# Products of ones in TensorE's first waits, bias and sink products later, and one rounding moved on ScalarE, in an encoder block

## The reference

```
h = modulate(rmsnorm(x, g0), sh1, sc1);  x = x + 0.5 * g1 * swiglu(h, w_ffn1_in, w_ffn1_out)
h = modulate(rmsnorm(x, g1), sh2, sc2);  x = x + g2 * (concat(hgrn2(h), attention(h)) @ w_mix_out)
h = modulate(rmsnorm(x, g2), sh3, sc3);  x = x + 0.5 * g3 * swiglu(h, w_ffn2_in, w_ffn2_out)
```

## Time and profile before

| | |
|---|---|
| median of 3 runs | 1033.9 us |
| lowest and highest | 1032.92 and 1034.93 us |
| the profiled execution | 1033.38 us |
| its span, first to last instruction | 1031.6 us |
| TensorE matmul busy | 1012.9 us, 98% |
| TensorE weight loads busy | 897.5 us, 87% |
| VectorE busy | 802.1 us, 78% |
| ScalarE busy | 507.8 us, 49% |
| GpSimd busy | 44.2 us, 4% |

### The profile page before, as it was taken

How to read it: one execution, slowest core, us unless ns; L and a number is a source line. 1 busy time by engine, 2 the same in 40 slices (tenths; PEclk the granted TensorE clock), 3 DMA queues, 4 the chain that set the end, 5 groups by cost and what they waited for, 6 DMA issues and landing times.

```text
span 1031.6 us, 16712 instructions
## 1 busy us (share of the span) xinstructions
PE 1012.9 (98%) x6238; PEld 897.5 (87%) x6238; DVE 802.1 (78%) x1189; ACT 507.8 (49%) x782; POOL 44.2 (4%) x32
## 2 busy tenths in 40 slices
PE   5999999999999999999999999999999999999998
PEld 3788999999888888888888888887999999988887
DVE  6889989988988789878788649578988888746533
ACT  4646555555222354683526773454655555532231
POOL 0000000000000050000200000420000000000000
PEclk9999999999999999999999999999999999999999
DMA  9643434343777442832120031222233332363312
GB/s 344 235 163 123 136 110 141 106 159 126 289 279 246 165 163 82 268 100 83 41 72 31 2 83 41 82 82 82 87 117 101 102 121 82 124 245 128 116 41 82
DMA packets 93811, 133.59 MB, mean 130 GB/s; under 512 B 10786, under 2 KB 77214, under 8 KB 93639
## 3 DMA queue, kind: packets, MB, share of 16 engines
q1 hardware_dynamic: 93438, 130.83, 37.9%
q10 hardware_dynamic: 328, 2.17, 0.6%
HBM read 130.88 MB, written 4.21 MB: 131 GB/s over the span
## 4 chain that ended last, share of the span: by engine, by line
PE 87%; DVE 7%; POOL 2%; DMA 2%; ACT 1%; issue 1%; SPq 0%; POOLq 0%; DVEq 0%; ACTq 0%
PE bank L2038 13%; PE bank L2039 13%; PE bank L2040 13%; PE bank L2286 11%; PE bank L2285 11%; PE bank L2284 11%; PE bank L2388 2%; DVE w_lo L1252 2%; PE bank L2489 2%; PE bank L2582 1%; PE bank L2475 1%; PE bank L2175 1%; DVE tmod L1336 1%; PE bank L2161 1%; PE bank L2167 1%; PE bank L2464 1%
## 5 line engine op out<-in xcount | busy, mean ns | idle before, releaser
L755 ACT ACTIVATE w_hi<-w_raw 128x2048 fp32r<-128x2048 f32 x47 | 89.9, 1913 | 202.1 <-PE bank L2040 191.2
L1252 DVE TENSOR_TENSOR w_lo<-w_raw,w_hi 128x2048 fp32r<-128x2048 f32 x47 | 109.5, 2330 | 94.7 <-ACT w_hi L755 94.7
L2284 PE MATMUL bank<-t_hi,left_hi 128*128 128x256 f32 x544 | 154.0, 283 | 0.0
L2285 PE MATMUL bank<-t_lo,left_hi 128*128 128x256 f32 x544 | 154.0, 283 | 0.0
L2286 PE MATMUL bank<-t_hi,left_lo 128*128 128x256 f32 x544 | 153.9, 283 | 0.0
L2038 PE MATMUL bank<-a_hi,w_hi 128*128 128x512 f32 x352 | 137.7, 391 | 0.3 <-DVE w_lo L1252 0.3
L2040 PE MATMUL bank<-a_hi,w_lo 128*128 128x512 f32 x352 | 137.0, 389 | 0.0
L2039 PE MATMUL bank<-a_lo,w_hi 128*128 128x512 f32 x352 | 137.0, 389 | 0.0
L2038 PE MATMUL bank<-h_hi,w_hi 128*128 128x512 f32 x336 | 133.3, 397 | 0.8 <-DVE w_lo L1252 0.8
L2040 PE MATMUL bank<-h_hi,w_lo 128*128 128x512 f32 x336 | 130.9, 390 | 0.0
L2039 PE MATMUL bank<-h_lo,w_hi 128*128 128x512 f32 x336 | 130.8, 389 | 0.0
(11 more groups left out here) (313 smaller groups left out, 1898.2 us busy)
## 6 DMA issues: line engine op xcount, KB each, us to landing
w_raw<-in_w_ffn_in SPq DMA_DIRECT2D x42, 1024.0 KB, 4.9
ada<-in_w_ada SPq DMA_DIRECT2D x24, 1024.0 KB, 5.0
w_raw<-in_w_ffn_out SPq DMA_DIRECT2D x22, 1024.0 KB, 4.9
w_raw<-in_w_mix_in SPq DMA_DIRECT2D x11, 1024.0 KB, 5.1
shift_in<-in_w_ada SPq DMA_DIRECT2D x4, 1024.0 KB, 8.3
ada_row<-in_w_ada SPq DMA_DIRECT2D x8, 512.0 KB, 4.1
scale_in<-in_w_ada SPq DMA_DIRECT2D x4, 512.0 KB, 6.8
x_nat<-in_x SPq DMA_DIRECT2D x2, 1024.0 KB, 8.6
```

The source lines that it names most:

```text
L755: sc.activation(w_hi[n % 2][:], src[:], ACT.Copy).then_inc(whi_done, 1)
L1252: ve.tensor_tensor(w_lo[n % 2][:], src[:], as_f32(w_hi[n % 2][:]), ALU.subtract).then_inc(wlo_done, 1)
L2284: te.matmul(into, wh, xh[:, k, :], start=(opens and k == 0), stop=False, skip_group_check=True)
L2285: te.matmul(into, wh, xl[:, k, :], start=False, stop=False, skip_group_check=True)
```

## The change

It has three parts.

1. A function `spin(n)` on TensorE multiplies the tile of ones by itself, the moving side repeated to 512 columns, n times into bank 6, whose content nobody reads. It is called with 2 at the start (after `ones` is filled), with 7 after the transpose of c, with 3 between the first and second token halves of x's transposes, and with 4 ahead of xn's transposes: 16 float32 products in all.
2. The bias and sink products move from ahead of xn's transposes to behind the products of the first two tiles of h. The wait for the copy of bank 0 (`vec_step`) goes, since the sink product now writes to columns 480 to 487 of bank 7. The transposes of xn 3 and x 2 now stand ahead of the second column sums, and these wait for the copied sink.
3. On ScalarE the rounding of the first half of weight tile 0 stands ahead of `evac_x(0)`, and the copy to `sink_b` moves behind `first_t(1)`.

```diff
--- before.py
+++ after.py
@@ -409,6 +409,7 @@
         def sum_bank(u):
             return bank[u]
 
+        SINK_SUM = bank[7][:, 480:480 + QH]
         LOW_D = 6
         LOW_BANK, CROSS_BANK = bank[LOW_D], bank[7]
 
@@ -802,15 +803,15 @@
             sc.activation(rms0[:, 1, :], rms0[:, 0, :], ACT.Sqrt, bias=eps_t[:], scale=1.0 / D).then_inc(norms[0].rt, 1)
             a.wait_ge(norms[0].rinv, 1)
             sc.activation(xn[:, 0, :], x_nat[:, 0, :], ACT.Copy, scale=rms0[:, 2, 0:1]).then_inc(norms[0].rt, 1)
-            a.wait_ge(sink_step, 1)
-            sc.activation(sink_b[:], bank[0][:, 0:QH], ACT.Copy).then_inc(sink_step, 1)
-            evac_x(0)
             a.wait_ge(first_ready[6], 16)
             sc.activation(w_hi[0][:, 0:4 * 2 * P], w_first[0][:, 0:4 * 2 * P], ACT.Copy).then_inc(first_split, 1)
+            evac_x(0)
             first_hi(0)
             first_hi(1)
             first_t(0)
             first_t(1)
+            a.wait_ge(sink_step, 1)
+            sc.activation(sink_b[:], SINK_SUM, ACT.Copy).then_inc(sink_step, 1)
             a.wait_ge(bias_mm, 1)
             sc.activation(row8[:], bank[3][0:QH, :], ACT.Copy).then_inc(rowpad_done, 1)
             evac_x(1)
@@ -2104,8 +2105,16 @@
                                     start=True, stop=True)
                 ins.then_inc(nm.wsum, 1)
 
+            def spin(n):
+
+                for _ in range(n):
+                    te.matmul(bank[6][:], ones[:], ones[:].unsqueeze(1).to_broadcast([P, 4, P]), start=True, stop=True)
+
+            pe.wait_ge(pool_set, 2)
+            spin(2)
             pe.wait_ge(consts_loaded, 32)
             te.transpose(bank[2][:, 0:DT], c_row[:], ident[0:DT, 0:DT]).then_inc(c_step, 1)
+            spin(7)
 
             def turn(dst, src, d, rows=range(TT)):
                 for t in rows:
@@ -2134,14 +2143,11 @@
             turn(bank[1], x_nat, 0, (0, 1))
             pe.wait_ge(c_step, 2)
             turn(bank[2], x_nat, 1, (0, 1))
+            spin(3)
             pe.wait_ge(x_loaded[1], 16)
             turn(bank[1], x_nat, 0, (2, 3)).then_inc(x_tr, 1)
             turn(bank[2], x_nat, 1, (2, 3)).then_inc(x_tr, 1)
-
-            pe.wait_ge(bias_consts, 48)
-            pe.wait_ge(vec_step, 2)
-            te.matmul(bank[3][0:QH, :], relb[:], table[:], start=True, stop=True).then_inc(bias_mm, 1)
-            te.matmul(bank[0][:, 0:QH], ones[0:1, :], sink_r[:], start=True, stop=True).then_inc(sink_step, 1)
+            spin(4)
             pe.wait_ge(norms[0].rt, 2)
             for rows_done, part in ((1, (0, 1)), (2, (2,)), (3, (3,))):
                 pe.wait_ge(xn_done, rows_done)
@@ -2176,18 +2182,21 @@
                                         start=False, stop=(k == DT - 1))
                 return ins
 
-            pe.wait_ge(sink_step, 2)
             pe.wait_ge(xT_act, 1)
             pe.wait_ge(first_split, 1)
             hi_hi(0, (0, 1))
             pe.wait_ge(first_split, 2)
             lo_hi(0, (0, 1))
             hi_lo(0, (0, 1))
-            column_sums(16, quarter_acc[1], 2, 2)
+            pe.wait_ge(bias_consts, 48)
+            te.matmul(bank[3][0:QH, :], relb[:], table[:], start=True, stop=True).then_inc(bias_mm, 1)
+            te.matmul(SINK_SUM, ones[0:1, :], sink_r[:], start=True, stop=True).then_inc(sink_step, 1)
             pe.wait_ge(norms[0].t, 1)
             turn_xn(3)
             pe.wait_ge(norms[0].t, 2)
             turn_x(2)
+            pe.wait_ge(sink_step, 2)
+            column_sums(16, quarter_acc[1], 2, 2)
             hi_hi(0, (2, 3))
             lo_hi(0, (2, 3))
             hi_lo(0, (2, 3))
```

## The result

| | before | changed |
|---|---|---|
| median | 1033.99 us (20 runs) | 1035.32 us (20 runs) |
| ratio | | 1.0013, 95% interval 1.0007 to 1.0019 |
| profiled execution | 1033.38 us, span 1031.6 | 1035.02 us, span 1033.2 |

The changed kernel is 1.3 us slower: less than the 0.2% that the forecast called the bound, but clear of the interval. The forecast was 1035.0. As the experiments show, part of that agreement is luck: one term was too small, and something that I had not seen gave 0.6 us back. One further execution of the kernel before, beside e1 to e4, took 1249.7 us at a mean granted clock of 0.76 and is left out of all figures.

What follows compares the result with a forecast made beforehand. TensorE, busy for 98% of the span, was taken to bound the kernel. At ScalarE's first tile of h, 16.7 + r/2 + 1.4 - 18.65 with r = 3.3 gave +1.1 us: 1035.0 us, range 1032.4 to 1037.4.

Steps and rivals of the forecast that it cites:

- The price of a product: One product of ones on TensorE takes 0.86 us at the high clock level, 1.72 at the low.
- the queue: TensorE works in order; 16 products (13.76 us) and 1.8 to 1.9 of transposes and sums precede xn's transposes.
- the sum: Delay of ScalarE's first tile of h: 16.7 + r/2 + 1.4 - 18.65 = r/2 - 0.55 us.
- r = 3.3: Microseconds from TensorE's first product of ones to the clock's rise; bounded by 1.4 and 8.1, giving +1.1 us.
- the rival of a late rise: Clock rises late, felt in the second block ahead of rows' transpose; decides from r = 5.2, 1036.9 at 8.1; chance 0.16.
- my case: The forecast proper: r from 1.4 to 5.2, first tile of h +0.15 to +2.07 us; chance 0.67.
- One for one to the end: One microsecond at the first tile of h (18.65) counts as one microsecond at the kernel's end.
- The hidden costs: Delays of c's and rows' transposes, bias and sink products cost nothing; without cover 0.2 us for c, 1.3 for bias and sink.
- The rounding: First weight tile rounded ahead of evac_x(0) frees ScalarE at 17.5; greatest gain 1.15 us, here nothing since TensorE's transposes end later.
- Hidden delay: Rival: clock rises almost at once or products cost less; TensorE meets ScalarE at 17.5, 1032.2 to 1033.4; chance 0.16.
- Transposes at the low level: Rival: xn's ten transposes still take 2.34 us rather than 1.35, sum +2.1, 1035.5; chance 0.02.
- Ones that never raise the clock: Rival: products of ones stay at the low level, xn's transposes start at 33.5, +17 us, 1050.6; chance 0.02.

Runs made afterwards that it cites:

- e1: Changed kernel with all 16 products of ones left out, the moves kept; 1033.91 us against 1033.88 for the kernel before, ratio 1.0002.
- e4: Kernel before with only the rounding of the first half weight tile put ahead of evac_x(0); 1033.73 us against 1033.88, ratio 0.9999.
- e2: Changed kernel with 2+4+2+2 products of ones in place of 2+7+3+4; 1032.68 us against 1033.88 for the kernel before, ratio 0.9988.
- e3: Kernel before with the 16 products of ones at the same four places, nothing moved; 1037.36 us against 1033.88, ratio 1.0034.
- e7: Changed kernel again, unaltered, for a second profile; 1035.05 us.
- e11: Changed kernel with one more product of ones behind the second column sums; 1034.09 us against 1033.56 for the kernel before, ratio 1.0004.
- e5: e2 with one more product of ones behind the second column sums; 1031.35 us against 1033.98 for the kernel before, ratio 0.9975.
- e6: e2 with evac_x(0) ahead of the rounding again; 1033.49 us against 1033.98 for the kernel before, ratio 0.9997.
- e9: Kernel before with ten float32 products of 8 columns behind the transpose of c; 1033.66 us against 1033.56, ratio 0.9998.

## Why the prediction was right, and where it wasn't

- **The price of a product and the queue** held. Products at the high level run 0.86 us apart (3.44 for the last four), the order of TensorE's queue sets the first tile of h, and e1, e2 and e3 fit no other of the readings that I had. The constant of the sum was 0.2 us too large: 16.7 + r/2 + 1.4 gives 21.1, 21.0 and 20.0 for r = 5.98, 5.77 and 3.72 (changed, e7, e11), measured 20.86, 20.76 and 19.81.
- **r = 3.3 was mis-sized.** The products of ones took 3.7 to 6.0 us to raise the clock in the seven profiles that have them from the start (changed 5.98, e7 5.77, e5 5.48, e2 4.91, e6 4.68, e3 3.79, e11 3.72). Four of these have the same nine products first and still spread from 3.7 to 6.0, so the kernel does not set r alone. In both profiled executions of the changed kernel r is above 5.2 and the tile 2.2 and 2.1 us later than in the first profile of the kernel before, not 1.1: they lie where I had put the rival of a late rise, which had 0.12 against 0.67 for my case. The bounds of 1.4 and 8.1 held. The Trainium skill (TensorE: Matmul & The Clock Gate, The HAM clock gate) says that the watch over activity runs free of the kernel's start; the spread of r is in keeping with it.
- **One for one to the end** held from 26.63 to 600 us (573.4 us in both) and failed at 700: 0.6 us came back through the fetch of code, in no case of mine. I had named a hole behind 27 that changes its length as what would break it; it did. For the two first profiles the account closes: 1.1 forecast, 1.3 more for r, 0.2 less for the constant, 0.6 less for the fetch, which makes the 1.6 us between them. That errors of opposite sign partly cancel is luck.
- **The clock stays up once it has risen** was taken for granted. It falls back in 13 of 20 executions of the changed kernel. Where it kept up, the changed kernel has a median of 1034.92, else of 1035.47; the kernel before has 1033.06 to 1033.36 and 1034.48 to 1034.71 in the three sets of runs beside the experiments. So the change costs 1.6 to 1.9 us in the first kind and 0.8 to 1.0 in the second; the measured 1.3 lies between. That the changed kernel loses the clock at a price of 0.6 us and the kernel before at 1.3 to 1.4, no run explains.
- **The hidden costs:** c's transpose at 4.85 cost VectorE nothing (5.60 against 5.66); the bias and sink products at 24.69 cost no more than 0.1 us in the hole, but only because the clock is up (e1: 1.2 us at the column sums); xn is complete 0.8 us later than before (17.49 against 16.72), and TensorE comes later still, as foreseen for a late rise. The moves turn waits of 1.63 us ahead of the column sums and 0.29 ahead of tile 2 into a single one of 1.22 ahead of tile 2. That they gain nothing there was right; that the clock can fall in such a wait, before and after the change, I had not asked.
- **The rounding** gains nothing in the kernel before (e4), and in the changed one ScalarE waits 2.88 us behind it anyway, as said; it is worth half a microsecond in e2 (e6).
- **The rivals.** Hidden delay: it takes fewer products, e2 and e5. Late rise: so it was in both profiles of the changed kernel. Transposes at the low level: excluded, 1.47 us for twelve at 19.57. Ones that never raise the clock: excluded.

## What to carry to other kernels

Work that only keeps TensorE's clock up stands in its queue like any other: give each wait just what fits in it, by the price of one product at both levels and the latest rise, and check in the timeline that the next real work still waits for its data. Here ten products in four waits gained and sixteen lost. Work moved into a wait must fit there at the low level too, unless something has raised the clock first (e1). The wait that matters for the clock may come after the first rise: one product in a wait of 1.2 us was worth 1.3 us, as much as the start with its ten (1.2).

## What the runs showed of the hardware

- Waits of TensorE of 1.2 us (e6) and 2.3 and 2.2 us (e3, e9), with transposes and one-column products beside them, were followed by 3.4 us at the low level. By the mean clock the executions of one kernel split into those with such a fall and those without.
- With the same nine products of ones first, the clock rose 3.7 to 6.0 us behind the first of them (changed, e7, e3, e11).
- A 16 KB fetch of TensorE's program on q8 beside a 1 MB load went with a load of 6.0 to 6.4 us instead of 4.9 to 5.0, and twenty to sixty-seven records more at the start went with a chain 0.6 us shorter, 640 us later.
- The last rows of x are first used anywhere between 12.0 and 13.8 us in these profiles; a comparison of two single profiles at that place is no better than this.
